# Delta-rule layer of a two-block transformer kernel: tap on ScalarE, weight rounding placed ahead, inverses woven with later projections

## What is computed

```python
def _gated_deltanet(h, w_in, conv_w, a_log, dt_bias, norm_w, w_out):
    proj = h @ w_in                       # 1024 -> 3072 (q, k, v) + 1024 (z) + 8 (a) + 8 (bb)
    qkv = jax.nn.silu(_causal_depthwise_conv(proj[..., :n_qkv], conv_w))   # 4 taps per column
    z = proj[..., n_qkv:n_qkv + GDN_V_WIDTH]
    a, bb = proj[..., -16:-8], proj[..., -8:]
    q = _l2norm(q of qkv) * (GDN_DK ** -0.5); k = _l2norm(k of qkv); v = v of qkv
    beta = jax.nn.sigmoid(bb)
    g = -jnp.exp(a_log) * jax.nn.softplus(a + dt_bias)
    o = _chunk_gated_delta_rule(q, k, v, g, beta)    # triangular solves with I + strict(K K^T * beta * decay)
    o = o * lax.rsqrt(jnp.mean(o * o, axis=-1, keepdims=True) + RMS_EPS)
    return (o * norm_w * jax.nn.silu(z)) @ w_out
```

## Time and profile before

| | |
|---|---|
| median of 3 runs | 2119.86 us (2115.82 to 2120.2) |
| the profiled execution | 2112.11 us, its span 2110.3 us |
| busy: TensorE, VectorE, ScalarE, GpSimd | 90%, 54%, 43%, 16% of the span |
| granted TensorE clock, mean | 0.941 of full speed |
| the layer's projections and inverses, from its first projection matmul to the first of the rule's chunks | 1237.81 to 1476.79 us |

### The profile page before, as it was taken

How to read it: one execution, slowest core, us unless ns; L and a number is a source line. 1 busy time by engine, 2 the same in 40 slices (tenths; PEclk the granted TensorE clock), 3 DMA queues, 4 the chain that set the end, 5 groups by cost and what they waited for, 6 DMA issues and landing times.

```text
span 2110.3 us, 29067 instructions
## 1 busy us (share of the span) xinstructions
PE 1901.6 (90%) x12225; PEld 1637.0 (78%) x12225; DVE 1130.2 (54%) x1579; ACT 907.0 (43%) x1396; POOL 345.0 (16%) x396
## 2 busy tenths in 40 slices
PE   5889878999999999968899978898799999999999
PEld 2756657888887888746799868788699978768997
DVE  2455547556574545574455556743455555565554
ACT  3443345344455444633454435432344444434443
POOL 2120222211241212120211120031200005200000
PEclk9899888999999999988999988998999999999999
DMA  8454453454656666320656533310245554504553
GB/s 275 140 202 140 160 179 124 157 170 158 204 171 202 216 226 210 126 80 11 209 180 189 181 100 111 115 54 1 96 159 180 189 170 173 176 1 140 180 184 135
DMA packets 217966, 320.61 MB, mean 152 GB/s; under 512 B 8550, under 2 KB 123946, under 8 KB 217452
## 3 DMA queue, kind: packets, MB, share of 16 engines
q1 hardware_dynamic: 212628, 308.96, 44.8%
q0 software_dynamic: 1744, 6.03, 0.8%
q10 hardware_dynamic: 3464, 3.75, 0.5%
HBM read 317.68 MB, written 1.05 MB: 151 GB/s over the span
## 4 chain that ended last, share of the span: by engine, by line
PE 74%; DVE 12%; ACT 6%; DMA 4%; POOL 2%; issue 2%; SPq 0%; POOLq 0%; ACTq 0%; DVEq 0%
PE ps L69 71%; DVE WLO L86 3%; PE ps L77 3%; DVE AR L96 2%; ACT WHI L80 1%; DVE AR L86 1%; DMA RAW<-in_w_mod_dram 1%; DMA RAW<-in_w_up_dram 1%; DMA RAW<-in_w_in_dram 1%; ACT AR L80 1%; POOL SM L86 1%; DVE SM L99 1%; ACT XR L80 1%; ACT L80 1%; POOL XR L86 1%
## 5 line engine op out<-in xcount | busy, mean ns | idle before, releaser
L86 DVE TENSOR_TENSOR WLO<-RAW,WHI 128x1024 fp32r<-128x1024 f32 (+2 forms) x506 | 593.8, 1215 | 426.8 <-ACT WHI L80 426.6
L80 ACT ACTIVATE WHI<-RAW 128x1024 fp32r<-128x1024 f32 (+2 forms) x506 | 488.2, 1014 | 396.0 <-PE ps L69 287.1
L69 PE MATMUL ps<-TH,WHI 128*128 128x256 f32 x1672 | 485.0, 290 | 27.1 <-DVE WLO L86 15.8
L69 PE MATMUL ps<-TL,WHI 128*128 128x256 f32 x1672 | 479.5, 287 | 0.0
L69 PE MATMUL ps<-TH,WLO 128*128 128x256 f32 x1672 | 479.3, 287 | 0.0
L69 PE MATMUL ps<-WHI,ARR 128*128 128x512 f32 x1120 | 355.6, 394 | 5.6 <-DVE ARR L86 3.1
L69 PEld LDWEIGHTS ps<-TH,WHI 128*128 128x128 f32 x1672 | 327.3, 196 | 38.5 <-issue 24.7
L69 PEld LDWEIGHTS ps<-TL,WHI 128*128 128x128 f32 x1672 | 327.3, 196 | 0.3
L69 PEld LDWEIGHTS ps<-TH,WLO 128*128 128x128 f32 x1672 | 326.7, 195 | 0.2
L69 PE MATMUL ps<-WHI,TH 128*128 128x512 f32 (+2 forms) x608 | 240.3, 395 | 24.1 <-DVE WLO L86 22.8
L69 PEld LDWEIGHTS ps<-WHI,ARR 128*128 128x128 f32 x1120 | 211.0, 188 | 56.8 <-issue 9.3
(11 more groups left out here) (187 smaller groups left out, 1947.7 us busy)
## 6 DMA issues: line engine op xcount, KB each, us to landing
RAW<-in_w_mod_dram SPq DMA_DIRECT2D x48, 1024.0 KB, 5.4
RAW<-in_w_up_dram SPq DMA_DIRECT2D x48, 1024.0 KB, 5.4
RAW<-in_w_down_dram SPq DMA_DIRECT2D x48, 1024.0 KB, 5.2
RAW<-in_ffn_w_in_dram SPq DMA_DIRECT2D x44, 1024.0 KB, 5.1
RAW<-in_w_in_dram SPq DMA_DIRECT2D x20, 1024.0 KB, 5.3
RAW<-in_ffn_w_out_dram SPq DMA_DIRECT2D x20, 1024.0 KB, 5.0
RAW<-in_dil_w_in_dram SPq DMA_DIRECT2D x18, 1024.0 KB, 4.8
RAW<-in_gdn_w_in_dram SPq DMA_DIRECT2D x16, 1024.0 KB, 5.8
```

The lines of the kernel that those rows point to most:

```text
L69: return Made(None if self.eng is None else self.eng.matmul(o, l, r, start=start, stop=stop))
L80: return Made(None if self.eng is None else self.eng.activation(o, i, f, **k))
L86: return Made(None if self.eng is None else self.eng.tensor_tensor(o, a, b, op))
```

## The change

1. `use` takes `own`: the narrow tile of the decays gets two parts of the small buffer `JK` as its rounded parts, and no turn in the two rounding buffers. `due` and `held` replace the count of tiles by the count of turns.
2. The fourth tap moves to ScalarE: `act_conv` copies a half of the bank to the row buffer and then writes the same half, scaled with the tap's weight, to the place of the result. VectorE adds the other three taps, its six operations alternating between the two halves.
3. The rounding leaves `act_conv` and `dve_conv`. `act_rest` and `dve_rest` now go through all twelve projections: in step n they round for the next projection, then do the copies or taps of projection n-1, then (ScalarE) the SiLU of n-2.
4. The decays are spread over steps 0 to 6. The keys' norms come after steps 4, 5 and 6, and the inverses are woven with the rest from step 7 on: projections 3 and 8 to 11, z, the queries' norms and the operands.
5. One exponential in `act_gates_of_rule` stands before the logarithm, the addition for the decays stands in `dve_abturn`, and `dve_sums` is cut in two.

```diff
-        def use(name, idx, k0, nk, c0, n, split=True):
+        def use(name, idx, k0, nk, c0, n, split=True, own=None):
...
+                    t.own, t.turn = own is not None, turns[0]
+                    if t.own:
+                        t.hi, t.lo = own
+                        t.turn -= 1
+                    else:
+                        s = t.turn % NW
+                        t.hi, t.lo = WHI[:, 2048 * s:2048 * s + 2048], WLO[:, 2048 * s:2048 * s + 2048]
+                        turns[0] += 1
...
+        def due(j, now):
+            return j < len(split_tiles) and split_tiles[j].turn <= now.turn + 1 and lands(split_tiles[j], now)
...
-            t = use("gdn_w_in_2", 0, 0, 8, 4096, 16)
+            t = use("gdn_w_in_2", 0, 0, 8, 4096, 16, own=(JKR[:, 0:128], JKR[:, 128:256]))
...
         def act_conv(c):
-            act_splits(tile_of["gdn_w_in_2", 0, 0, 256 * c])
...
+                act.act(raws_of(cc)[:, 3:259], v, ACT.Copy)
                 said = [("free", (("qkv", c), 0))] if f == 1 else []
-                act.act(raws_of(cc)[:, 3:259], b[:, 256 * f:256 * f + 256], ACT.Copy).then_inc(act_gd, ("raw", cc), *said)
+                act.act(QKV[:, cc, :], v, ACT.Copy, scale=CWv[:, 3, cc:cc + 1]).then_inc(act_gd, ("raw", cc), *said)
...
         def dve_conv(c):
-            dve_splits(tile_of["gdn_w_in_2", 0, 0, 256 * c])
-            for f in range(2):
-                cc = 2 * c + f
-                q, r = QKV[:, cc, :], raws_of(cc)
-                dve.wait_ge(act_gd, ("raw", cc))
-                dve.ts(q, r[:, 0:256], CWv[:, 0, cc:cc + 1], None, ALU.mult).then_inc(dve_gd, ("conv", cc, 0))
-                for w in range(1, 4):
-                    dve.wait_ge(dve_gd, ("conv", cc, w - 1))
-                    dve.stt(q, r[:, w:w + 256], CWv[:, w, cc:cc + 1], q, ALU.mult, ALU.add).then_inc(dve_gd, ("conv", cc, w))
+            for w in range(3):
+                for f in range(2):
+                    cc = 2 * c + f
+                    q = QKV[:, cc, :]
+                    dve.wait_ge(act_gd, ("raw", cc))
+                    if w:
+                        dve.wait_ge(dve_gd, ("conv", cc, w - 1))
+                    dve.stt(q, raws_of(cc)[:, w:w + 256], CWv[:, w, cc:cc + 1], q, ALU.mult, ALU.add).then_inc(dve_gd, ("conv", cc, w))
...
         def act_rest():
-            for c in REST:
-                act_conv(c)
-                act_convsilu(c)
+            def after(n):
+
+                if 0 <= n - 1 < 12:
+                    act_conv(CONVS[n - 1])
+                if 0 <= n - 2 < 12:
+                    act_convsilu(CONVS[n - 2])
+            for n in range(12):
+                act_splits(conv_tile(n))
+                if n == 5:
+                    act_sums()
+                after(n)
+                if n == 2:
+                    act_gates_of_rule()
                 yield
...
-        def gdn(step):
...
-            weave((inv, 20), (rest, 24))
+        def gdn(k, rest, inv):
+
+            for x in 5 * [rest] + 3 * [k] + [rest] + 2 * [k] + [rest] + 4 * [k]:
+                next(x, None)
+            weave((rest, 22), (inv, 20))
```

More of the change, by code:

```diff
@@ L356, in halves_of, with held @@
             return ((0, 0, n // 2), (1, n // 2, n))
+        def held(t):
+            return next((x for x in split_tiles if not x.own and x.turn == t.turn - NW), None) if not t.own else None
+        def due(j, now):
+            return j < len(split_tiles) and split_tiles[j].turn <= now.turn + 1 and lands(split_tiles[j], now)
         def lands(w, t):
@@ L363, in act_splits @@
         def act_splits(now):
-            while act.j <= min(now.j + 1, len(split_tiles) - 1) and lands(split_tiles[act.j], now):
+            while due(act.j, now):
                 t = split_tiles[act.j]
+                had = held(t)
                 for h, a, b in halves_of(t):
                     act.wait_ge(w_land[t.i % NRAW], t.i)
-                    if t.j >= NW:
-                        act.wait_ge(pe_gemm, ("used", split_tiles[t.j - NW].i))
+                    if had is not None:
+                        act.wait_ge(pe_gemm, ("used", had.i))
                     act.act(t.hi[:, a:b], t.raw[:, a:b], ACT.Copy).then_inc(act_w, ("hi", t.i, h))
@@ L374, in dve_splits @@
         def dve_splits(now):
-            while dve.j <= min(now.j + 1, len(split_tiles) - 1) and lands(split_tiles[dve.j], now):
+            while due(dve.j, now):
                 t = split_tiles[dve.j]
@@ L2537, in pe_rest @@
         def pe_rest():
-            for c in REST:
+            for n, c in enumerate(CONVS):
                 pe_conv(c)
+                if n == 0:
+                    pe_ab()
+                elif n == 1:
+                    pe_abturn()
+                elif n == 4:
+                    pe_sums()
                 yield
@@ L2562, in act_rest @@
             for c in range(2):
-                for _ in act_rows(("z", c), z_spec(c), TLS, act_z(c)):
+                for i, _ in enumerate(act_rows(("z", c), z_spec(c), TLS, act_z(c))):
+                    if c == 0:
+                        after(12 + i)
                     next(qn, None)
@@ L2569, in dve_rest @@
         def dve_rest():
-            for c in REST:
-                dve_conv(c)
+            for r in RAWSb:
+                dve.memset(r[:, 0:3], 0.0).then_inc(dve_gd, "pads")
+            for n in range(12):
+                dve_splits(conv_tile(n))
+                if n == 1:
+                    dve_ab()
+                elif n == 2:
+                    dve_abturn()
+                elif n == 5:
+                    dve_sums()
+                elif n == 6:
+                    dve_ratesums()
+                if n >= 1:
+                    dve_conv(CONVS[n - 1])
+                if n == 3:
+                    dve_gates_of_rule()
                 yield
@@ L2581, in pool_rest @@
         def pool_rest():
-            for c in REST:
+            for _ in CONVS:
                 yield
@@ L2789, in act_gdn @@
         def act_gdn():
[L2790 to L2796 removed]
+            gdn(act_l2(8), act_rest(), act_inverses())
             act_chunks()
```

62 lines of the change are left out of this document (18 added, 44 removed).

## The result

The changed kernel takes **2091.41 us** (median of 4 runs, 2089.13 to 2094.09) against 2120.03 for the kernel before (4 runs, 2115.82 to 2120.57). The ratio is 0.9873, with a 95% interval of 0.9858 to 0.9887. That is 28.6 us faster, against a forecast of 28.

What follows compares the result with a forecast made beforehand. The ring of taps, SiLU, rounding and `WLO` bounds the stage's first half, mostly TensorE's matmuls the second. Work of 180.9 plus losses of 28.2 gives 209.1 for 239.0; less 2 for masks, 28 us gained: 2092, range 2077 to 2107.

Steps and rivals of the forecast that it cites:

- The opened ring: Projections: taps, SiLU, rounding, `WLO`, taps no longer wait in a circle; rounds go from 7.66 to TensorE's 5.8 us.
- keys' squares: Step 5: ScalarE waits for sums and loads tables twice, the keys' fourth square comes late; 0.8 us lost.
- sums and K K^T: Setup of the inverses: TensorE waits about 2.6 us at the sums.
- bank of the fourth turn: Setup of the inverses: TensorE waits 2.4 us for the bank of the fourth turn.
- low clock behind it: After the fourth turn's wait, matmuls run slower; 5.3 us lost, priced from a c and a z step before.
- operands: Operand stretch: waits of 1.2 to 1.9 us and low clocks behind them stay unchanged; 15.3 us lost.
- masks on GpSimd: GpSimd's masks fall among roundings and taps; 2 us lost (0 to 6).
- Tap and order: Projections: VectorE needs 4.8 us each, below TensorE's 5.83; two scaled copies on ScalarE take 0.7 and cost nothing.
- Decays: Step 2: exponentials, logarithm and two table loads of 1.28 put ScalarE about 2 us behind; it catches up.
- the rival built on it: Slower tables: each load delays what follows by twice the 1.28; gain 21, 2099 us; chance 0.03.
- Inverses earlier: Inverses placed between projections: no matmuls removed, setup waits of 2.6 and 2.4 us plus 5.3 for a low clock.
- VectorE the bound?: Rival: VectorE bounds the interleaved part, each GpSimd mask costing it 0.7; gain 12, 2108 us; chance 0.17.

Runs made afterwards that it cites:

- changed_again: The changed kernel, unaltered, run and profiled once more on another chip: 2090.63 us, ratio 0.987.
- shared_narrow: Changed kernel with the decays' narrow tile back in the two shared rounding buffers: 2087.97 us, ratio 0.9856.
- operand_banks: Changed kernel with the operands' products and sums in the four banks of `gring` instead of three shared with the inverses: 2073.07 us, ratio 0.9789.
- taps4: Changed kernel with the fourth tap back on VectorE, everything else as changed: 2088.85 us, ratio 0.9866.
- late_taps4: Changed kernel with the fourth tap back on VectorE and all twelve projections ahead of the inverses, ring open: 2083.98 us, ratio 0.9842.
- late_inverses: Changed kernel with all twelve projections before the first step of the inverses: 2091.49 us, ratio 0.9863.

## Why the prediction was right

The mechanism, the stage and the time came out as forecast: 2091.41 for 2092, with the stage at 212.35 for 209 to 212. The opened ring is what the runs confirm; the close agreement of the number is partly luck, as the table shows. Term by term, the measured values are differences of starts in the changed kernel's rows, less the same work at the full clock.

| Term | Forecast | Measured | From |
|---|---|---|---|
| first projection at the low clock | 1.8 | 2.2 | 1243.84 to 1251.91 = 8.07, less 5.83 |
| keys' squares | 0.8 | 0.3 | wait of 0.27 |
| one projection behind them | 0 | 1.5 | 1288.65 to 1295.96 = 7.31, partly at the lower level |
| sums and K K^T | 2.6 | 3.5 | 1305.28 to 1315.59 = 10.3, for 8 x 0.85 |
| bank of the fourth turn | 2.4 | 2.3 | wait of 2.30 |
| low clock behind it | 5.3 | 1.1 | 1331.72 to 1338.69 = 6.97 |
| low clock without a wait | 0 | 3.2 | 1379.46 to 1389.06 = 9.60, for 6.4 |
| operands | 15.3 | 15.0 | 43.84, less 29.4 from the version with four banks; and 0.6 ahead |
| masks on GpSimd, and not assigned | 2 | 2.3 | what is left of 212.35 |

The measured terms before the last add up to 29.1, with 180.9 of work to 210.0. **The sum held partly because two errors cancelled.** The low clock behind the fourth turn was priced by a c step and a z step of the earlier trace rows, and what stood behind the wait here was a projection, of which only a part ran at the lower level: 1.1 for 5.3. About the same amount was lost at two places that the prediction did not name (1.5 and 3.2). Both come back in the second profile of the changed kernel, and neither is there when the fourth tap stands on VectorE, though nothing but that differs: the prediction had no way to see them.

*Tap and order.* Projections are 5.8 us apart (three in 17.38, 1260.71 to 1278.09), the taps 0.41 each, the scaled copies 0.7 for two: all as taken, and the ring was the right thing to look at. Its size beside the other parts was not asked for in the prediction, and it is not one number: opening the ring brings some 9 us with the inverses woven early and 28 to 30 with them late. The step that had the wrong weight is the tap: the prediction counted the 4.8 us of VectorE against 5.83 and did not ask whether 5.3, with the tap left there, would do as well. It does.

*Decays.* The loads cost nothing beyond their 1.28: the next operation began 1.29 later (1263.95 to 1265.24). The 2.66 us of the Trainium skill, ScalarE: Activation LUTs, What ACT_TABLE_LOAD costs, are not seen here either; the trace disagrees with the drain behind a load, and the rival built on it falls.

*Inverses earlier.* The waits it puts in the setup were foreseen to within 1 us (two of 1.36, one of 2.30). The prediction gave this part no gain, which was right beside an open ring; that it brings 12 to 14 us beside a closed one, by filling its gaps, was not said.

*VectorE the bound?* No: over the stage it has 124 us of work for 212, and the one crowded place cost what is in the table. One GpSimd mask beside the taps did cost 1.03 (3.49 for 2.46), more than the 0.7 of the rival. The mask's own row is the clearer one, on GpSimd in the changed kernel:

```profile
1318.25 3.34 POOL L86 TENSOR_TENSOR XN<-AR,CF 128x512 f32<-128x512 f32 x1 [3.11 <-DVE AR L96]
```

It took 3.34 in place of 1.29. The two `WLO` halves beside its first 2.2 us were not slowed at all (2.35), and the taps behind them were held for 1.03. So the two engines took turns: GpSimd stood until VectorE's pair was done, and then VectorE stood. The Trainium skill, SBUF — State Buffer, Who interferes with whom, has this as an exclusive lock on the one pair of ports that VectorE and GpSimd share; by that rule, the trace agrees.

*Operands.* The pattern stayed, as forecast, at 15.0 for 15.3. That this was the largest loss left can be read from the prediction's own terms. That it came from the banks, and not from data on the way, only the run with four of them showed.

## What to carry to other kernels

Draw the ring of engines round one step before counting any engine's work: the order of two steps on two queues (rounding ahead of taps, SiLU one round later) was worth up to 30 us here, while the instruction that was moved to a less busy engine made no difference that the times show. Parts of a change can stand in for each other: what fills gaps is worth 12 to 14 us while the gaps are there and nothing when they are gone, so each part is measured with the others in and with them out. Before two programs that are woven together share a ring of banks, look at what the engine that frees a bank has in front of that work, and give a stretch of short round trips all the banks that lie idle. When two kernels differ, look for the places: a third of the 30 us between the closed and the open ring lay where the two do the same work, at another clock.

## What the hardware showed that was not expected

- The granted clock fell without any gap. From 1356.00 to 1379.00 TensorE was busy for all 23.00 us at 1.00, and from 1379.46 on a c step took 4.69 and the z step behind it 5.15, at a mean of 0.64 (the stretches of the changed kernel above), before 1.00 came back at 1389. The rows before it are z matmuls, norms and steps of the inverses, without a wait (the ends of matmuls are modelled in the profile, so very short gaps could hide). It is no accident of one execution: `changed_again`, `shared_narrow` and `operand_banks` have a mean of 0.64 in the same 9.6 us, each on the same step. With only the tap moved back (`taps4`) the clock stays at 1.00 there. What brought it down is open.
- Short waits can go with a lower clock, and the same waits need not. At the operands of the changed kernel four banks took away 6 us of waits and brought 14.4, the granted clock rising from 0.82 to 1.00. But in `late_taps4` and `late_inverses` waits of the same kind, up to 1.24 us, are all there, and the clock is 1.00 over the 55.72 us that both take from their first wait at the operands on; in the two early kernels with the closed ring it is 0.92.
- The same instructions do not meet the same clocks from run to run. In the first 100 us, where the two kernels are equal, their profiled executions have 0.94 and 0.86 (before) and 0.90 and 0.83 (after) for each 50 us, and a second profile of the changed kernel has 0.92 and 0.87. The start of the stage lies anywhere in 8 us over the profiles; that this comes from those clocks is likely and was not shown.
